# Moving the output gates' projections of a hybrid mixer behind each head's q, k and v

## The reference

```python
proj = h @ w_in
gu, gv, q, k, v, gate, b_logit, a_logit = split_cols(proj, IN_SIZES)
y_a = chunk_spatial_gating(gu, gv, gm_ln_g, gm_ln_b, gm_ws, gm_bs)
qkv = jax.nn.silu(causal_dwconv(jnp.concatenate([q, k, v], axis=-1), dn_conv))
q, k, v = split_cols(qkv, (DN_QK, DN_QK, DN_V))
q, k = l2norm(q), l2norm(k)                       # per head, 4 heads of 128
beta, g = sigmoid(b_logit), -exp(a_log) * softplus(a_logit + dt_bias)
o = gated_delta_rule(q, k, v, g, beta)
o = rmsnorm(o, dn_onorm) * jax.nn.silu(gate)
return jnp.concatenate([y_a, o], axis=-1) @ w_out
```

## Time and profile before

| | |
|---|---|
| median of 3 runs | 1616.75 us (1615.31 to 1617.93) |
| the profiled execution | 1615.61 us, its span 1613.8 us |
| PE busy | 1573.3 us, 97% of the span |
| DVE, ACT, POOL busy | 874.9, 586.0, 135.5 us |
| mean granted clock of PE | 0.991 |

### The profile page before, as it was taken

The page is one execution under the profiler, slowest core; times in us unless marked ns, Lnnn a source line. Parts: engine busy times, 40 slices in busy tenths (PEclk is TensorE's granted clock), DMA queues, the critical chain, the costliest instruction groups (busy, mean ns, idle before and its releaser), DMA issues.

```text
span 1613.8 us, 20684 instructions
## 1 busy us (share of the span) xinstructions
PE 1573.3 (97%) x8314; PEld 1302.4 (81%) x8314; DVE 874.9 (54%) x1286; ACT 586.0 (36%) x870; POOL 135.5 (8%) x122
## 2 busy tenths in 40 slices
PE   9799999999999999999999999999999999999997
PEld 7678778887778888888887878778888888888887
DVE  6666664653445444344556576644555663564565
ACT  5533333443344233231552333433333432332232
POOL 0120210210011000000044001000002000000000
PEclk9899999999999999999999999999999999999999
DMA  6111112532113323222322232232233223223221
GB/s 256 41 52 53 53 54 66 177 123 79 52 65 105 105 92 98 97 94 84 118 91 79 65 105 65 92 105 72 85 118 103 80 95 107 91 99 105 92 69 63
DMA packets 45022, 147.18 MB, mean 91 GB/s; under 512 B 5120, under 2 KB 8320, under 8 KB 44800
## 3 DMA queue, kind: packets, MB, share of 16 engines
q1 hardware_dynamic: 43200, 142.91, 26.9%
q10 hardware_dynamic: 1728, 2.95, 0.5%
HBM read 143.75 MB, written 2.10 MB: 90 GB/s over the span
## 4 chain that ended last, share of the span: by engine, by line
PE 84%; DVE 6%; issue 4%; ACT 3%; POOL 1%; DMA 1%; SPq 0%; POOLq 0%; DVEq 0%; ACTq 0%
PE bank L1229 25%; PE bank L1230 25%; PE bank L1231 25%; DVE temp L1757 1%; PE bank L1424 1%; PE bank L1441 1%; PE bank L1149 1%; ACT w_hi L1507 1%; POOL square_sum L2186 1%; DVE temp L1750 1%; PE bank L1156 1%; PE bank L1366 1%; PE bank L1338 1%; PE bank L1371 0%; PE bank L1194 0%
## 5 line engine op out<-in xcount | busy, mean ns | idle before, releaser
L1229 PE MATMUL bank<-a_hi,w_hi 128*128 128x512 f32 (+1 forms) x1283 | 506.4, 395 | 0.3 <-DVE a_lo L1777 0.3
L1230 PE MATMUL bank<-a_lo,w_hi 128*128 128x512 f32 (+1 forms) x1283 | 496.3, 387 | 0.0
L1231 PE MATMUL bank<-a_hi,w_lo 128*128 128x512 f32 (+1 forms) x1283 | 496.2, 387 | 0.0
L1765 DVE TENSOR_TENSOR w_lo<-w_raw,w_hi 128x1024 fp32r<-128x1024 f32 (+1 forms) x260 | 334.6, 1288 | 173.8 <-ACT w_hi L1507 173.4
L1507 ACT ACTIVATE w_hi<-w_raw 128x1024 fp32r<-128x1024 f32 (+1 forms) x260 | 268.2, 1034 | 217.4 <-PE bank L1231 205.5
L1229 PEld LDWEIGHTS bank<-a_hi,w_hi 128*128 128x128 f32 x1283 | 243.0, 189 | 53.5 <-issue 4.7
L1231 PEld LDWEIGHTS bank<-a_hi,w_lo 128*128 128x128 f32 x1283 | 243.1, 190 | 49.2
L1230 PEld LDWEIGHTS bank<-a_lo,w_hi 128*128 128x128 f32 x1283 | 243.4, 190 | 47.3 <-issue 1.2
L1229 PE MATMUL bank<-b_hi,w_hi 128*128 128x512 f32 (+1 forms) x720 | 276.6, 384 | 0.4 <-ACT b_hi L1640 0.4
L1230 PE MATMUL bank<-b_lo,w_hi 128*128 128x512 f32 (+1 forms) x720 | 275.1, 382 | 0.0
L1231 PE MATMUL bank<-b_hi,w_lo 128*128 128x512 f32 (+1 forms) x720 | 275.1, 382 | 0.0
(11 more groups left out here) (296 smaller groups left out, 1227.9 us busy)
## 6 DMA issues: line engine op xcount, KB each, us to landing
w_raw<-weights_in SPq DMA_DIRECT2D x248, 512.0 KB, 3.3
w_raw<-weights_in SPq DMA_DIRECT2D x8, 384.0 KB, 3.0
x_first<-x_in SPq DMA_DIRECT2D x8, 256.0 KB, 6.5
xs<-x_in ACTq DMA_DIRECT2D x8, 256.0 KB, 5.8
w_raw<-weights_in SPq DMA_DIRECT2D x8, 256.0 KB, 2.5
out<-xs SPq DMA_DIRECT2D x16, 128.0 KB, 1.9
mem_x<-mem_in SPq DMA_DIRECT2D x1, 1024.0 KB, 9.5
w_raw<-front_in SPq DMA_DIRECT2D x5, 192.0 KB, 6.6
```

Source lines behind the costliest of these rows:

```text
L1229: pe.matmul(to, weights_hi[:, at], hi, start=k == k0, stop=False)
L1230: pe.matmul(to, weights_hi[:, at], lo, start=False, stop=False)
L1231: t = pe.matmul(to, weights_lo[:, at], hi, start=False, stop=k == k1 - 1)
L1765: dve.tensor_tensor(lo[:, 0:size], raw[:, n % SLOTS, 0:size], hi[:, 0:size].bitcast(F32), ALU.subtract).then_inc(split_dve.handle, 1)
```

## The change

`head_gate(h)` is new: it lets head h into the delta rule and projects its gate. It is called for head 0 behind the v of head 1, for head 1 behind that of head 2, for head 2 behind that of head 3, and for head 3 behind gu 0 and gv 0. `scaled(h)` (behind the sums) no longer lets the head in. Within a head, the steps keep their order, and the decays stay the first of them. The steps of the memory norm, formerly between the gates, follow gv 1, 2 and 3. On POOL the two strict instructions run where the list has `turn`.

```diff
--- before.py
+++ after.py
@@ -66,11 +66,13 @@
             add("qkv", part * H + h)
             if h == part == 0:
                 add("logits", 0)
+        if h:
+            add("gate", h - 1)
     for n in range(H):
         add("gu", n)
         add("gv", n)
-    for n in range(H):
-        add("gate", n)
+        if n == 0:
+            add("gate", H - 1)
     for name in ("xa_wk", "xa_wv", "w_out", "xa_wq", "xa_wo"):
         for n in range(KT):
             add(name, n)
@@ -234,7 +236,6 @@
 
     def scaled(h):
         add("norms", h)
-        normed_heads.append(h)
 
     def projections():
         for h in range(H):
@@ -244,6 +245,9 @@
             aside.extend([lambda: None] * (3 if h == 0 else 1))
             aside.extend([lambda h=h: add("sums", h), lambda h=h: scaled(h)])
             yield from conv_qkv(2 * H + h)
+            if h:
+                yield from head_gate(h - 1)
+        norm = memory_norm()
         for n in range(H):
             yield from halves_and_aside("gu", n)
             add("spatial_u", n)
@@ -252,16 +256,20 @@
             add("spatial_v", n)
             aside.extend([lambda n=n: add("statistics", n), lambda n=n: add("normalise", n), lambda n=n: add("mix", n)])
             yield
-        norm = memory_norm()
-        for n in range(H):
-            if n != 1:
+            if n == 0:
+                yield from head_gate(H - 1)
+            else:
                 next(norm, None)
-            yield from halves_and_aside("gate", n)
-            add("gate", n)
-            yield
         while aside:
             aside.pop(0)()
             yield
+
+    def head_gate(h):
+
+        normed_heads.append(h)
+        yield from halves_and_aside("gate", h)
+        add("gate", h)
+        yield
 
     def memory_norm():
         for t in range(KT):
@@ -2209,7 +2217,7 @@
                 elif kind == "statistics":
                     q.wait_ge(*statistics_dve.at(n))
                     power(ln_mean[n % 2][:, :, 1], statistics_pool)
-                elif kind == "strict":
+                elif kind == "turn":
                     q.wait_ge(*consts_landed.at(4))
                     q.wait_ge(*strict_dve.at(n, 3))
                     pool.tensor_tensor(level_b[n % 2][1][:, :, :], strict_b[n % 2][:, :, :], over_tokens(half_matrix(1), NC), ALU.mult
```

## The result

The changed kernel takes 1622.13 us (median of 8 runs, 1619.32 to 1623.46), the kernel before 1616.8 us beside it (8 runs, 1615.31 to 1620.31): a ratio of 1.0031, 95% interval 1.0022 to 1.0041. It is slower by some 5 us. The runs of one kernel differ by up to 7 us. The profiled execution took 1622.91 us with a span of 1621.2.

What follows compares the result with a forecast made beforehand. PE, busy 97% of the span, was taken as the bound. Gaps of 21.8 for 20.4 us (+1.4) and clock of 7.2 for 4.0 gave +4.6 on 1615.6: 1620.2, or 1621 on the median; eight-in-ten range 1612.5 to 1627.

Steps and rivals of the forecast that it cites:

- Heads 0 and 1: PE's waits for these heads' inverse blocks: 1.2 us for 9.77 at turn 0, 0 for 2.30 at turn 1.
- The new wait at sums 1: PE waits 2.6 us for the square of k of head 1; bounds 0 and 3.8 (one whole convolution).
- Heads 2 and 3: PE's waits: 2.4 us for 0.41 at turn 2, 1.7 for 2.04 at turn 3, 0.5 at solve 1.
- Memory norm: Its eight squares block ACT ahead of the normalise that frees a bank; PE waits 4.7 us for 2.92.
- The end: End of the delta rule, from gv 3's last half to xa_wk: 8.7 us idle for 2.24, no projections left.
- The walk of 19.7 us: Chain of steps from gv 3's last half to the first xa_wk matmul, with PE's own pieces 11.0 us.
- the tail's waits under 6 us in sum: Sign that would show the prediction wrong, for waits between gv 3 and xa_wk.
- The clock: Falls to PE's lower clock cost 7.2 us for 4.0 before (ends 1.6 and 12), 3.2 in the tail.
- the first xa_wk matmul: First PE matmul after the delta rule: expected near 267.3 us, breaking even at 262.7.
- Rival 1: The clock does not fall in the tail and at turn 2: +0.6 us, 1617.4; chance 0.28.
- rival 3: Lower clock through the whole tail: 4 to 6 us more, 1627; decides if tail exceeds 23 us; chance 0.09.
- The falls that I counted by it: A fall after every gap over 2 us, three in the tail: six falls, 9.6 us, giving 1619.4.

Runs made afterwards that it cites:

- after_spread: The changed kernel with the memory norm's eight squares issued in pairs instead of one burst; 1615.71 us (ratio 0.999).
- after_fill: The changed kernel with 24 matmuls of overwritten result added on PE ahead of mix 3, solve 3 and state 0; 1617.09 us (1.0009).
- late23: The changed kernel with gates 2 and 3 projected behind gv 3 again, all head entries left late; 1614.9 us (0.999).
- entry_only: The changed kernel with all four gates projected behind gv 3 again, heads still entering late; 1627.33 us (1.0073).
- gates_only: The changed kernel with gates kept early, but heads entering right behind their norms as in the kernel before; 1613.44 us (0.9985).
- before_spread: The kernel before with only the memory norm's eight squares issued in pairs instead of one burst; 1616.18 us (1.0002).
- turn_later2: gates_spread with head 0's turn coming two half projections later; 1607.01 us (0.9947).

## Why the prediction was right, and where it was not

**The time**, 1621 us, stands beside 1622.13, and the direction, slower by more than 0.2%, was right. Its parts were right in unequal measure.

**Heads 0 and 1.** Turn 0's wait was forecast at 1.2 and measured 0.99, turn 1's at 0 and is 0. The new wait at sums 1 was forecast at 2.6 and is 4.24, outside the bound of 3.8. The square came when the walk said (the wait ends at 59.25, forecast 59.8), but PE was ready at 55.0, not at 57.2: the walk took PE's place from an execution whose clock was 0.91 between 40 and 60 us, and in this one it was 0.98. In after_spread and after_fill, where it is 0.91 again, the wait is 2.8 to 2.9, and in late23, where it is 0.83, 1.24. So this term was right to 0.3 us at the clock that it was worked out from, and its bound was wrong because it left PE's clock out.

**Heads 2 and 3.** Forecast 2.4, 1.7 and 0.5; measured 2.03, 0.64 and 0.80 (the 12.5 of the first adds up to 12.4, which changes nothing). The gap of 0.71 went.

**Memory norm.** 4.7 forecast, 4.58 measured, and after_spread shows the cause that the prediction names. What it left out is that the wait costs more than its length: over 6 us in the runs, since the clock falls behind it (0.83).

**The end.** The walk of 19.7 us without the clock's share is confirmed by after_fill: 3.3 us from the start at 245.92 to the matmul at 249.24, and 16.1 from there on, 19.4. PE's idle time in it is 5.8 us by the rows, not 8.7, which meets one of the prediction's own signs of being wrong (the tail's waits under 6 us in sum). About half of the difference is the low clock, which stretches PE's own pieces over part of the waits: in after_fill, at the higher clock, the waits (0.48, 0.25, 0.72) and the filler (some 5.8) take 7.3 us together, and PE's own pieces 12.1 where the walk had 11.0.

The reason that the prediction gives ("before, the gate halves lay between these steps") is the step that failed. The halves do cover the end (24.2 us without them, 15.0 in entry_only), but their move isn't what makes the kernel slower: entry_only has the gate halves behind gv 3 again and is slower still, and gates_only has them early and is faster than the kernel before. The prediction costed the gates and the entries as one move; it is the later entries that lose. How they do it is shown only in part. With them the last solve stands behind all 47 halves and not behind 44, so that the recurrence has nothing beside it; but this count doesn't decide alone, since with all 47 the last xa_wv matmul comes between 324.98 (after_spread) and 338.22 us (entry_only), and in entry_only the waits for a normalise (9.8 us) are twice those of its end (0.52, 1.79, 1.71 and 0.71 us).

**The clock.** This is the mis-sized term: 7.2 us forecast for the whole stretch (ends 1.6 and 12), 3.2 of it for the end. The end took 4.8 by after_fill. For the whole, the gaps of the changed kernel sum to 0.99 + 4.24 + 2.03 + 0.64 + 0.80 + 4.58 + 5.8 = 19.1 us against 20.4 before, where I had forecast 21.8; yet the landmark is 7.5 us later. 7.5 + 1.3 = 8.8 us more of slow clock than before, against 3.2 forecast: 12.8 in all with the 4.0 of before, a little over the upper end. This 8.8 is a remainder and not a reading; by the page PE is busy 7.3 us longer for the same matmuls, and idle as long as before. So it is 7.3 to 8.8 more, and 11.3 to 12.8 in all. The gaps came out 2.7 us too long and the clock 5.6 too short in the forecast; the first xa_wk matmul was expected at 267.3 and came at 270.15, and the difference of 2.9 is these two. Part of it is that one execution: it lies 0.8 us above the median of the changed kernel, and that of before 1.1 under its own. So the prediction was right in its time by luck in part: two terms erred to opposite sides. Rival 1, no fall at the end, is refuted, and rival 3 (decides over 23 us of the end) had its deciding point reached, at 24.2 us, without its time of 1627: of the 4.8 us that the low clock took at the end, the forecast already held 3.2.

The Trainium skill (TensorE: Matmul & The Clock Gate, section "Why this matters for your kernels") says to leave no long idle gap between bursts of matmuls. The trace agrees as far as the end goes: with the gaps filled the clock stays at 1.00, and unfilled it falls; but none of the four gaps there is longer than 2.26 us, so that here several short ones were enough. The falls that I counted by it, three at the end (4.8 us) and six in all (9.6 us), came nearer to what was found (4.8; 11.3 to 12.8) than my own (3.2 and 7.2); the time made from them, 1619.4, was too low as well.

**A version that beats both.** gates_spread, with the gates early as in the change, the heads entering right behind their norms as before, and the squares in pairs, takes 1607.89 us against 1616.53 of the kernel before: 0.58% less (0.9942, 0.993 to 0.9955), and 0.9% less than the changed kernel.

**Open.** Why the squares in pairs gain nothing in the kernel before and 5 to 6 us with the gates early is seen only as other gaps and a fall of the clock; no run takes it apart. Late entries with the gates late and the squares in pairs (entry_only with the edit of after_spread) weren't run, so how much of the 11 to 12 us of entry_only is the squares' move stays open. The gap of 9.7 us at turn 0 is open too: three ways to remove it or fill it were tried, and none gained a measurable time over gates_spread.

## What to carry to other kernels

Where chains are threaded through a fixed stock of filler work, count how much filler is left when the last chain ends: a chain that enters later to spare a wait at its front can pay for it further on. Move one thing at a time: here two moves in one change were worth about -0.15% and +0.73% by themselves, each with the squares' move in it. A burst on an engine with idle time (ACT, 36% busy) can be the dearest thing in a stretch if what others wait for is queued behind it, and a gap in PE can cost more than its length, by a slower clock behind it (4.58 us of gap, over 6 of time).

## What the runs showed that I had not expected

- The slower clock at the end costs 4.8 us for 5.8 us of gaps, and 24 useless matmuls save 3.6 to 5 us (after_fill).
- The wait of 4.58 us is followed by a clock of 0.83; without it the time falls by over 6 us (after_spread). A wait of 2.62 us in before_spread was followed by 0.91, one of 2.04 at the same turn in the kernel before by 1.00.
- The page's idle time of PE didn't change at all (40.5 and 40.6 us) in a kernel that got 5 to 7 us slower.
- Gaps wander: of 9.72 us removed at turn 0, 5.7 reappeared at sums 1 and turn 2 (turn_later2).
